# Modulation row sums moved under the output projection, which starts on eight of its sixteen K-tiles; one mixer half's head norms put ahead of its gates

## What is computed

```python
mod = c_act @ w_ada[l] + b_ada[l]
sh_m, sc_m, gt_m, sh_f, sc_f, gt_f = jnp.split(mod[:, None, :], N_MOD, axis=-1)
h = rmsnorm(x, pre_mix_norm[l]) * (1.0 + sc_m) + sh_m
proj = h @ w_in[l]
o_hg = hgrn2_group(proj[..., :HG_COLS], lb_all[l], hg_norm[l])     # 8 heads, decay by log f
o_gdn = gdn_group(proj[..., HG_COLS:], ...)                        # 8 heads, triangular inverse
y = jnp.concatenate([o_hg, o_gdn], axis=-1) @ w_out[l]
x = x + gt_m * rmsnorm(y, post_mix_norm[l])
h = rmsnorm(x, pre_ffn_norm[l]) * (1.0 + sc_f) + sh_f
...
# both groups end so:  o = rmsnorm(o, norm_w) * jax.nn.silu(g_out)
```

## Time and profile before

| | |
|---|---|
| median of 3 runs | 2971.63 us (2969.46 to 2971.84) |
| the profiled execution | 2972.81 us, its span 2970.9 us |
| PE busy | 2706.9 us, 91% of the span |
| DVE, ACT busy | 1816.4 us (61%), 1225.9 us (41%) |
| mean granted TensorE clock | 0.962 of 2.4 GHz |
| first mixer, from the last in-projection matmul to unit 0 of the output projection | 463.6 to 708.0 us |

### The profile page before, as it was taken

One profiled execution on the slowest core, in us unless ns is written; L12 is line 12 of the kernel. 1 busy time (PEld: TensorE's weight loads), 2 busy tenths in 40 slices (PEclk: granted clock), 3 DMA queues, 4 the chain that ended last, 5 costly groups with the idle time before them and its releaser, 6 DMA issues.

```text
span 2970.9 us, 32505 instructions
## 1 busy us (share of the span) xinstructions
PE 2706.9 (91%) x12554; PEld 2201.3 (74%) x12554; DVE 1816.4 (61%) x2165; ACT 1225.9 (41%) x1559; POOL 61.4 (2%) x84
## 2 busy tenths in 40 slices
PE   4899996687799999999988999997989999999987
PEld 2478885586678888888866877776778888878875
DVE  6678777775785555555664456567455565656455
ACT  2133444342444444444434444543544434344432
POOL 1000000000000000000001000000000000000000
PEclk8899999798999999999999999998999999999998
DMA  9978992044575555555654634444445656565552
GB/s 360 328 215 279 323 331 113 29 152 163 212 275 193 194 186 184 184 188 192 224 186 139 198 115 141 148 150 149 163 146 181 198 170 198 169 198 179 164 165 87
DMA packets 150718, 562.28 MB, mean 189 GB/s; under 512 B 9800, under 2 KB 14023, under 8 KB 146768
## 3 DMA queue, kind: packets, MB, share of 16 engines
q1 hardware_dynamic: 146512, 542.15, 53.5%
q0 software_dynamic: 3920, 18.22, 1.8%
q10 hardware_dynamic: 176, 0.40, 0.0%
HBM read 556.28 MB, written 4.46 MB: 189 GB/s over the span
## 4 chain that ended last, share of the span: by engine, by line
PE 52%; issue 32%; DVE 10%; ACT 4%; DMA 2%; POOL 1%; SPq 0%; DVEq 0%; POOLq 0%; ACTq 0%
PE banks L406 15%; PE banks L408 15%; PE banks L407 15%; PE banks L711 3%; DVE weights_low L364 2%; DMA raw_weights<-in_w_ada 2%; ACT weights_high L351 2%; PE banks L473 1%; DVE proj L1099 1%; DVE mod_in L796 1%; DVE proj L993 1%; POOL small L620 1%; DVE modulation L382 1%; DVE proj L977 0%; DVE y_rows L458 0%
## 5 line engine op out<-in xcount | busy, mean ns | idle before, releaser
L364 DVE TENSOR_TENSOR weights_low<-raw_weights,weights_high 128x1024 fp32r<-128x1024 f32 (+2 forms) x846 | 990.3, 1179 | 917.2 <-ACT weights_high L351 898.3
L351 ACT ACTIVATE weights_high<-raw_weights 128x1024 fp32r<-128x1024 f32 (+2 forms) x846 | 858.2, 1021 | 1022.5 <-PE banks L408 957.6
L406 PE MATMUL banks<-weights_high,lhs_high 128*128 128x512 f32 (+1 forms) x2208 | 877.4, 397 | 27.1 <-DVE weights_low L364 19.2
L408 PE MATMUL banks<-weights_high,lhs_low 128*128 128x512 f32 (+1 forms) x2208 | 861.5, 390 | 0.0
L407 PE MATMUL banks<-weights_low,lhs_high 128*128 128x512 f32 (+1 forms) x2208 | 860.3, 390 | 0.0
L406 PEld LDWEIGHTS banks<-weights_high,lhs_high 128*128 128x128 f32 x2208 | 417.7, 189 | 119.3 <-DVE weights_low L364 20.9
L408 PEld LDWEIGHTS banks<-weights_high,lhs_low 128*128 128x128 f32 x2208 | 416.9, 189 | 86.4
L407 PEld LDWEIGHTS banks<-weights_low,lhs_high 128*128 128x128 f32 x2208 | 418.0, 189 | 80.5 <-issue 0.5
L406 PE MATMUL banks<-weights_high,hid_high 128*128 128x512 f32 x856 | 337.6, 394 | 19.4 <-DVE hid_low L2400 9.8
L407 PE MATMUL banks<-weights_low,hid_high 128*128 128x512 f32 x856 | 335.3, 392 | 0.0
L408 PE MATMUL banks<-weights_high,hid_low 128*128 128x512 f32 x856 | 335.2, 392 | 0.0
(11 more groups left out here) (401 smaller groups left out, 2085.4 us busy)
## 6 DMA issues: line engine op xcount, KB each, us to landing
raw_weights<-in_w_ff SPq DMA_DIRECT2D x128, 1024.0 KB, 5.0
raw_weights<-in_w_in SPq DMA_DIRECT2D x96, 1024.0 KB, 5.5
raw_weights<-in_w_up SPq DMA_DIRECT2D x80, 1024.0 KB, 4.9
raw_weights<-in_w_ada SPq DMA_DIRECT2D x72, 1024.0 KB, 5.8
raw_weights<-in_w_down SPq DMA_DIRECT2D x42, 1024.0 KB, 5.1
raw_weights<-in_w_out SPq DMA_DIRECT2D x32, 1024.0 KB, 5.1
raw_weights<-in_w_ada SPq DMA_DIRECT2D x32, 768.0 KB, 8.4
first_weights<-in_w_in SPq DMA_DIRECT2D x16, 768.0 KB, 6.8
```

The costliest lines, as they stand in the source:

```text
L351: act.activation(WHI[:, u % SPN, 0:c.width], RAW[:, n % RAWN, k % 2, 0:c.width], ACT.Copy).then_inc(S("high_made"), 1)
L364: dve.tensor_tensor(WLO[:, u % SPN, 0:c.width], RAW[:, n % RAWN, k % 2, 0:c.width], WHI[:, u % SPN, 0:c.width].bitcast(F32), ALU.subtract) ...
L406: nc.tensor.matmul(o, x, hi, start=(k == 0), stop=False)
L408: mm = nc.tensor.matmul(o, y, hi, start=False, stop=(k == c.kn - 1))
```

## The change

Four things move. **Front:** the transposes of PA go into the last in-projection chunk, ahead of its unit 10 (`pe_in1_last`); the two modulation sums and ACT's two copies leave the head of the mixer. **Scans:** ACT signals after four of the eight logarithms, and DVE starts the scans of those heads then. **Heads ahead of gates:** on DVE `dve_heads` of hg comes before the gdn gate arithmetic. **Output projection:** PE turns only rounds 0 to 3 (tiles 0 to 7, the hg heads) ahead of unit 0. The gdn norm is cut up and hung between the splits of units 4 and 6 on DVE (its product with the norm weights goes into the first two inverse levels), and rounds 4 to 7 stand ahead of unit 7. The modulation sums of rows 0, 1 and 2 stand ahead of units 9, 11 and 13, all through banks 4 to 7, so that each waits for the reader of the one before. The `phases` table and the core of the rest:

```diff
+        def pe_in1_last(pe):
+            pe.wait_ge(S("narrow_taken"), 1)
+            hg_turn(pe, PA)
         def pe_mix1(pe):
             for b in range(4):
                 pe.wait_ge(S(f"bank_free{b}"), MIX1.at["done"][b])
-            pe.wait_ge(S("ada_used"), ADA_IN)
-            for b in range(8):
-                mm = nc.tensor.matmul(PS[:, b % 8, :], ONES, MOD[:, b // 4, 512 * (b % 4):512 * (b % 4) + 512],
-                                      start=True, stop=True)
...
+            pe.wait_ge(S("hg_gated"), 1)
+            hg_turn(pe, PQ)
...
-            pe_split(pe, "mix1", P, ready=(S("mix1_ready"), 1), wait=False)
+            pe.wait_ge(S("hg_out"), 2)
+            pe_split(pe, "mix1", P, 8, ready=(S("mix1_ready"), 1), wait=False)
         def act_mix1(act):
-            for comp in range(2):
-                act.wait_ge(S("mod_summed"), comp + 1)
-                act.activation(MOD[:, comp, :], bank_cols(4 * comp, 4), ACT.Copy).then_inc(S("mod_copied"), 1)
             act.wait_ge(S("hg_turned"), 1)
+            act.wait_ge(S("unit_used"), MIX1.at["u"])
             act.activation(LB[:, 2, :], bank_cols(4, 4), ACT.Sigmoid).then_inc(S("hg_gated"), 1)
...
-            last.then_inc(S("hg_logs"), 1)
+                if h % 4 == 3:
+                    last.then_inc(S("hg_logs"), 1)
...
+            last.then_inc(S("mix1_ready"), 1)
+            dve_split(dve, "mix1", LH2, LL2, 8)
+            dve.wait_ge(S("mix1_ready"), 1)
+            for t in range(TT):
+                last = dve.tensor_tensor(G0[:, t, :], F1[:, t, :], F1[:, t, :], ALU.mult)
...
+        def dve_gdn_scale(dve):
+            dve_rstd(dve, "gdn_heads", stat=STAT, n=DH)
...
+        def dve_gdn_gate(dve):
+            for t in range(TT):
+                last = dve.tensor_tensor(F1[:, t, :], F1[:, t, :], PG2[:, t, :], ALU.mult)
+            last.then_inc(S("mix1_ready"), 1)
+        def pe_gdn_split(pe):
+            pe_split(pe, "mix1", P, 8, ready=(S("mix1_ready"), 2), first=8, wait=False)
...
         def pe_mod_sum(pe, row, steps):
             pe.wait_ge(S("ada_used"), steps)
+            if row:
+                pe.wait_ge(S("mod_copied"), row)
+            else:
+                pe.wait_ge(S("round_free"), round_of["mix1"] + 8)
...
+        def dve_mod0(dve):
+            dve.wait_ge(S("vecs_in"), 32)
+            dve.wait_ge(S("mod_summed"), 1)
+            dve.tensor_tensor(MOD[:, 0, :], bank_cols(4, 4), VEC[:, :], ALU.mult).then_inc(S("mod_copied"), 1)
...
-                  ("mix1", dict(pe=tile_waits("mix1", (0, pe_mix1), (11, pe_mod2)), act=[None, act_mix1],
-                                dve=[None, dve_mix1] + [None] * 8 + [dve_mod2])),
+                  ("in1_last", dict(pe=[None] * 10 + [pe_in1_last])),
+                  ("mix1", dict(pe=tile_waits("mix1", (0, pe_mix1), (7, pe_gdn_split), (9, pe_mod0), (11, pe_mod1), (13, pe_mod2)),
+                                act=[None, act_mix1] + [None] * 4 + [act_gdn_split] + [None] * 4 + [act_mod1],
+                                dve=[None, dve_mix1, dve_gdn_scale, dve_gdn_gate] + [None] * 2 + [dve_gdn_split] + [None] * 2 +
+                                [dve_mod0] + [None] * 3 + [dve_mod2])),
```

More of the change, by code:

```diff
@@ L257, in block_pair @@
         segs = [(1, [in1(5, "conv0", None, 512), in1(6, "conv1", in_ada[6]), in1(7, "conv2", in_ada[7])] +
-                 [in1(j, None, in_ada[j]) for j in range(4)])]
+                 [in1(j, "in1_last" if j == 3 else None, in_ada[j]) for j in range(4)])]
         in_segs = len(segs)
@@ L1109, in conv_fns, with hg_turn @@
             return dict(pe=spread(pe_x), dve=spread(dve_x))
+        def hg_turn(pe, src):
+            for t in range(TT):
+                for h in range(H1):
+                    tr = nc.tensor.transpose(slot(t, h), src[:, t, 128 * h:128 * h + 128], IDENT)
+            tr.then_inc(S("hg_turned"), 1)
+        def pe_in1_last(pe):
+            pe.wait_ge(S("narrow_taken"), 1)
+            hg_turn(pe, PA)
         def pe_mix1(pe):
@@ L1313, in dve_mix1 @@
             link(last)
-            dve.wait_ge(S("hg_logs"), 1)
-            for g in range(TT * GRP // CH):
+            order = sorted(range(TT * GRP // CH), key=lambda g: (CH * g % GRP * 2 // GRP, g))
+            for n, g in enumerate(order):
                 gs = slice(CH * g, CH * g + CH)
+                if n % (len(order) // 2) == 0:
+                    dve.wait_ge(S("hg_logs"), 1 + 2 * n // len(order))
                 last = dve.tensor_tensor_scan(out=LB[:, 2, gs], data0=ONES[:, 0:CH], data1=LB[:, 3, gs], initial=0.0,
@@ L1342, in dve_mix1 @@
             last.then_inc(S("hg_out"), 1)
+            dve.wait_ge(S("hg_out"), 1)
+            dve.wait_ge(S("hg_gate"), 2)
+            straight(dve_heads(dve, link, "hg_heads", *([heads3(x, t) for t in range(TT)] for x in (PQ, F2, PG1)),
+                               ROWS[:, 0:128], H1, DH, STAT, S("hg_out")))
             dve.wait_ge(S("gate_exps"), 2)
```

52 lines of the change are left out of this document (28 added, 24 removed).

## The result

The changed kernel takes 2954.8 us (median of 5 runs, 2952.92 to 2957.54) against 2971.84 us of the kernel before in the same session (5 runs). The ratio is 0.9937, with an interval of 0.9927 to 0.9948: faster by 17.0 us, where 19.0 were forecast and 2952.6 us named.

A forecast was written before the change was run, and what follows sets the result against it. The mixer was taken as bound by a chain passing PE, ACT and DVE, with PE full before it; 7.1 + 2.0 + 9.6 + 0.3 = 19.0 us gave 2953.8 profiled, 2952.6 against the median; range 2945 to 2958.5.

The forecast's parts named there:

- Front: Mixer's head: with sums and copies gone and PA's transposes in the in-projection, the sigmoid starts sooner; gain 7.1 us.
- POOL's memset: In-projection: POOL's clearing of PA now falls under DVE's splits; priced at nothing, 0.85 us without cover.
- Scans: Mixer: DVE's scans start after four of eight logarithms and are never short of input; gain 2.0 us.
- Heads ahead of gates: Mixer: the second value transposes follow at once instead of waiting for DVE; gain 9.6 us, between 8.5 and 10.8.
- Norm products: Inverse levels: two DVE products of 1.22 us hidden in DVE's idle time; uncovered they would be 2.4.
- Output projection: Unit 0 starts 18.0 us earlier, but stalls, rounds, sums, a wait and the clock leave a gain of 0.3.
- The wait: Output projection: PE waits ahead of sum 1 for late-landing vectors, 5.1 us, bounds 3.6 to 8.
- the clock behind it: Output projection: a low clock after PE's wait at sum 1 loses 1.7 us, bounds 0 and 3.4.
- A: Rival: no wait at sum 1 of the output projection, 2945.8 us; chance 0.2.
- B: Rival: DVE bounds the output projection's first eight units, 3 to 6 us more, 2955.5 to 2959; chance 0.17.
- C: Rival: the new order of heads does nothing, because gates queued behind them hold PE; 2962 us; chance 0.04.
- D: Rival: slower, the vectors landing so late that the wait at sum 1 eats everything; about 2980 us; chance 0.03.

The follow-up runs named there:

- logs_whole: Changed kernel, but DVE's scans wait for all of ACT's logarithms instead of each half: 2954.9 us.
- gates_first: Changed kernel with the gdn gate arithmetic back ahead of the hg heads on DVE: 2964.8 us.
- act_row0: Changed kernel, but ACT copies sum 0 out of the banks and the product with `vec` moves behind the third sum: 2945.4 us.
- vec_first: Changed kernel with POOL's two vector loads issued ahead of the load of x: 2943.1 us.
- two_idles: Changed kernel with modulation sum 0 in PE's idle stretch at the mixer's head and sum 1 behind the decay loop, ahead of the norm products: 2941.8 us.
- idle_sums: Changed kernel with modulation sums 0 and 1 moved from the output projection into PE's idle stretches of the mixer's head: 2942.3 us.
- sums_front: Changed kernel with PA's transposes and the sums of rows 0 and 1 back at the mixer's head: 2944.9 us.
- both_fills: Changed kernel with twelve unread matmuls ahead of the decay loop's last scores and sixteen ahead of the norm products: 2951.1 us.

## Why the prediction was right, step by step

**Front**, 7.1: 7.16 measured. **POOL's memset** at no cost: it took 1.81 us at 448.16, and the split and the sums that DVE began at 447.54 and 448.68 took 1.23 and 2.60 us, as elsewhere. The 0.85 that the prediction named as the other outcome was not paid. **Scans**, 2.0: 1.97 where they stand. That a gain there also reaches the end was taken without a reason; it holds up to the tail (logs_whole: 1.97 later there), and the time doesn't show it.

**The decay loop's tail** has no term in the prediction. I had read a granted clock of 0.58 there and used it only to price another wait; that the same place could run at a low clock for longer was not considered. It cost 2.2 us between the two profiles, and with 17.84 of 19.0 us from the terms it is more than the whole miss: the others came out 1.0 better. That the profiled executions nevertheless differ by 18.6 us, 0.4 from the forecast, is in part luck: about 1 us was gained ahead of the change by nothing in it. Since the tail takes either value in kernels with the same code, whether it belongs to the 2.0 us by which the median missed stays open.

**Heads ahead of gates**, 9.6 (8.5 to 10.8): 10.0 by both traces and by gates_first, and 10.6 with what was gained up to the gdn output, where the gate rows took 4.48 us against 4.95: the sooner rise of the clock, which I had bounded at 1.2 and taken as 0. POOL's copy fell behind the products as foreseen (568.28, 2.01 us), where it had cost DVE 0.85 twice. **Norm products** in the inverse levels were hidden, as said.

**Output projection.** Unit 0 came 18.2 us sooner relative to the gdn output (forecast 18.0). PE waited 0.5 and 0.5 us ahead of units 5 and 6, not 1.1 and 0.9: mis-sized by 1.0, since, counted from unit 0, DVE had them 0.3 and 0.4 us sooner than reckoned, and PE came to unit 5 0.3 later. Rounds 4 to 7 took 1.9 (2.0). Two more sums 3.59 of PE each, as before's one. The wait 5.6 (5.1, bounds 3.6 to 8), the clock behind it 1.8 (1.7). The last vector landed at 711.35 on the time axis of after, where 730.1 less 18.6 is 711.5. Two misses meet in that: it was issued 0.6 sooner than reckoned (695.45), and it took 2.0 longer than before, not 1.5. What is left, 0.6 us, I don't assign to a row. The tail kept 0.3, as forecast.

**Rivals.** A (no wait, 2945.8) did not happen, but it is what act_row0 and vec_first give, 2945.4 and 2943.1. B did not happen: PE idled 1.0 us among the first eight units. C and D are out. What the cases had in common, that everything outside them stays as it is, was the weak point.

## What to carry to other kernels

When a change makes a wait for a load, look first at what the same queue issues ahead of it: one line moved was worth 7.3 us here, as much as the front had gained. Work that must be done somewhere belongs into an idle stretch of its engine inside the chain, with a free bank and a reader that is idle soon after; under a full projection its whole length is paid. And a gain of 2 us is to be followed from landmark to landmark, with its neighbours on and off: the earlier scans' 2.0 us were there up to the decay loop's tail, and one execution's clock in the tail hid them. Extra matmuls that held the clock up made them visible.

## What the runs showed of the hardware

**The clock's dips move.** The same instructions of the decay loop's tail ran for 3 to 10 us at a granted clock of 0.50, and the same code got either: L942 took 2.25 us before, in gates_first, logs_whole and two_idles, 3.77 in idle_sums, and 4.01 to 4.2 in the others without the twelve matmuls. Three us of matmuls in the idle stretch ahead kept it at 2.25 in all four kernels that had them. The Trainium skill (TensorE: Matmul & The Clock Gate, Part 1) says that the number of slow matmuls of one kernel varies from run to run; the traces agree, with 2.25 us in gates_first and 4.01 in the changed kernel, whose code is the same up to there. That an edit upstream changes it, beyond shifting when the matmuls come, is not shown.

**Executions differ outside the changed stretch in steps.** The code is the same in all fourteen kernels from the first y_rows on, but for a line or two, and yet the way from there to one of POOL's powers (L621, at 1538.90 in the profile of after) takes either 801.2 to 801.4 (seven kernels) or 802.8 to 803.0 (seven), and the last 770 us either 768.4 to 768.6 (vec_first, sums_front, gates_first) or 771.0 to 771.5 (the rest). The windows of the last two stretches of 60 us show that as granted clock, 0.91 and 0.84 in the profile of after, 0.94 and 0.86 in that of vec_first. The start of ACT's last weights_high varies too, from 465.0 us in the changed kernel to 471.2 in both_fills, with the same code ahead of it. Together that is several us that no edit made, a good part of the difference between the medians and the stretches above: a median of five runs tells 3 us poorly here. A short piece of the trace tells far less than 1 us (from the gdn output to the first y_rows the six kernels with the same code there take 67.98 to 68.26); the whole stretch of 270 us does not, because its tail alone moves by 2.5 us.

**GpSimd's copies and DVE slow each other**, 2.01 to 3.20 us and 2.36 to 3.91, and which DVE instructions they meet is set by PE's pace.
